# Query and key projections interleaved with windowed attention on one Trainium2 core

## The chip, the cores and the metric

The kernel runs on one core of one Trainium2 chip. Its engines are TensorE (PE in the rows: matmuls, with its weight loads as PEld), VectorE (DVE), ScalarE (ACT), GpSimd (POOL) and SyncE (SP), which here issues the DMA transfers. The metric is the device time of one execution in microseconds (us), the median of three runs.

## The reference

Two layers over 1024 latent tokens of width 1024, with 256 context tokens before them. The first layer is a gated convolution with a feed-forward part. The second is neighbourhood attention with 16 heads of width 64: the latent tokens form 16 rows of 64, and each query sees a window of 8 rows by 16 columns, with a learned bias, and all 256 context tokens.

```
qkv = hl @ w_qkv                      # 1024 latent tokens
kv_c = hc @ w_qkv[:, D:]              # 256 context tokens
...
s_win = einsum('bhqd,bhrqcd->bhqrc', q_r, k_win) * scale + bias
s_ctx = einsum('bhqd,bkhd->bhqk', q_r, k_ctx) * scale
p = softmax(concatenate([s_win, s_ctx], -1))
return einsum(p_win, v_win) + einsum(p_ctx, v_ctx)
...
yl = o @ w_o;  xl = xl + g1 * yl;  xl = xl + g2 * swiglu(...)
```

## The kernel before

Everything is float32 in and out. A projection splits weights and activations in a high and a low half and sums three products, so one output tile of 128 channels takes 8 blocks x 3 = 24 matmuls. Tokens come in tiles of 512, 512 and, for the context, 256 (`ALL`); `LAT` has the first two. The work runs in stages: modulation, convolution, feed-forward 0, then the second layer: values (`v_quarter`), queries and keys (`qk_step`), attention, output projection (`wo`), feed-forward 1.

Heads go in 8 pairs. `qk_step(i)` projects the queries (two tiles) and the keys (three tiles) of pair i, so a pair has 120 matmuls. ScalarE copies each tile out as its high half (`stage_q_hi`, `stage_k_hi`), VectorE subtracts for the low half, and SP stores both to `q_dram` and `k_dram`. All eight pairs are done before attention starts.

Attention of a pair has 8 units (four of each head; a unit is 256 queries). The keys of a unit stand in groups of 256 or less: units 0, 3, 4 and 7 have three groups, the others four, 28 in a pair, numbered here 0 to 27. Around a group TensorE does, in this order:

- in the first two groups of a unit, `scores` of the unit after the next (six matmuls),
- `turn` of the group two further on: three or four transposes of the probabilities into one of two banks; it waits for `pt_lo_done` of the group whose bank it takes,
- `values` of this group: four matmuls on `pt_hi` and `pt_lo`.

VectorE adds the bias to the scores and finds the minimum (`bias_scores`, two passes), ScalarE takes the exponentials (`probs`), VectorE inverts the sums, GpSimd multiplies (`probs` L1514), TensorE turns, ScalarE copies the high half (`pt_high`), VectorE makes the low half (`pt_low`). At the end of a unit ScalarE copies half the result (`half`), VectorE sums (`head_sum`, `sum_done`), and ScalarE and GpSimd write `o_hi` and `o_lo` (`out_high`, `out_low`) straight into the buffers that the output projection reads. The value products use banks 6 and 7 in turn, so those of a unit wait for the sum of the unit before the last.

Each engine runs its list in the written order and waits at semaphores in it. SP issues everything on one queue; `load_head(i, b)` brings the bias, queries, keys and values of one head. In its loop it waits until the scores and value products of that head of the pair before are done. The queue's order is therefore the order of the transfers.

```
def values(i, u, g):
    if g == 0:
        at_least(pe, sum_done, UNITS * i + u - 1)
```

## Time and profile before

| | |
|---|---|
| median of 3 runs | 3264.9 us (3263.08 to 3267.94) |
| the profiled execution | 3264.37 us, span 3262.6 us |
| busy: PE, PEld, DVE, ACT, POOL | 3023.7, 2499.6, 1752.1, 818.4, 741.0 us |
| instructions | 44434 |
| mean granted TensorE clock | 0.977 of full speed |
| values stage ends, q/k stage | 1758.5 us; 1759.5 to 1959.5 us |
| attention, first turn to last sum | 1985.8 to 2379.8 us |

The span is the profiled execution from its first instruction to its last. An engine is busy while an instruction of it runs; waits, branches and the issuing of DMAs don't count. In the rows, "idle before ... <-" is the time in which an engine stood still ahead of an instruction and what released it.

### The profile page before, as it was taken

The page shows a single profiled execution, that of the slowest core. Times are in us where ns is not written, and L with a number is a line of the kernel's source. Part 1 is how long each engine was busy: PE and PEld are TensorE (multiplying, and loading weights), DVE is VectorE, ACT ScalarE, POOL GpSimd, SP SyncE. Part 2 cuts the span into 40 slices and gives each one's busy share as a digit, 9 for nine tenths or more (in the row PEclk, how much of TensorE's full clock was granted, in tenths as well). Part 3 has the DMA queues.
Part 4 walks back from the last instruction along what each step waited for, and adds up shares of the span by engine and source line. Part 5 has one row for each costly group of instructions (what it writes and reads, how often), then busy time and mean ns, then how long its engine had stood idle before and what let it go on. Part 6 is the DMA issues. An engine that isn't in the chain of part 4 may idle for free. (4 is left out here: it accounts for less than half of the span.)

```text
span 3262.6 us, 44434 instructions
## 1 busy us (share of the span) xinstructions
PE 3023.7 (93%) x15712; PEld 2499.6 (77%) x15712; DVE 1752.1 (54%) x2975; ACT 818.4 (25%) x1412; POOL 741.0 (23%) x457
## 2 busy tenths in 40 slices
PE   5899999899999999999799996888898999999997
PEld 2688887578888888888499885777776888888885
DVE  1645555566677666644631115777724555555556
ACT  1311111411111111111231115777733111111112
POOL 0311211021111111111111214555531212121220
PEclk8999999999999999999999998999999999999999
DMA  9110103022221222111044327455320111111111
GB/s 350 70 52 26 51 26 87 1 73 72 77 77 54 77 72 72 63 39 39 13 101 123 139 113 159 112 118 127 81 72 13 58 39 58 39 58 39 58 39 58
DMA packets 171967, 243.97 MB, mean 75 GB/s; under 512 B 107904, under 2 KB 125312, under 8 KB 171904
## 3 DMA queue, kind: packets, MB, share of 16 engines
q1 hardware_dynamic: 171904, 243.14, 24.6%
q8 instruction: 38, 0.62, 0.1%
q14 instruction: 25, 0.20, 0.0%
HBM read 209.54 MB, written 37.49 MB: 76 GB/s over the span
## 5 line engine op out<-in xcount | busy, mean ns | idle before, releaser
L1148 DVE SCALAR_TENSOR_TENSOR residual<-psum,modulation,residual 128x512 f32<-128x512 f32 (+1 forms) x1072 | 718.1, 689 | 890.7 <-PE psum L557 889.4
L1458 POOL TENSOR_TENSOR w_lo<-raw,w_hi 128x1024 fp32r<-128x1024 f32 x196 | 491.0, 2517 | 2017.3 <-ACT w_hi L801 2017.3
L528 PE MATMUL psum<-act_hi,w_hi 128*128 128x512 f32 (+1 forms) x2528 | 676.7, 367 | 10.6 <-POOL w_lo L1458 7.6
L528 PE MATMUL psum<-act_lo,w_hi 128*128 128x512 f32 (+1 forms) x2528 | 676.7, 367 | 0.0
L528 PE MATMUL psum<-act_hi,w_lo 128*128 128x512 f32 (+1 forms) x2528 | 676.1, 367 | 0.0
L528 PEld LDWEIGHTS psum<-act_hi,w_hi 128*128 128x128 f32 x2528 | 453.5, 188 | 100.6 <-issue 7.8
L528 PEld LDWEIGHTS psum<-act_hi,w_lo 128*128 128x128 f32 x2528 | 436.4, 188 | 81.2
L528 PEld LDWEIGHTS psum<-act_lo,w_hi 128*128 128x128 f32 x2528 | 435.8, 188 | 81.5
L801 ACT ACTIVATE w_hi<-raw 128x1024 fp32r<-128x1024 f32 x196 | 203.9, 1061 | 1020.5 <-PE psum L528 964.1
L557 PE MATMUL psum<-prod_hi,w_hi 128*128 128x512 f32 (+1 forms) x1072 | 407.9, 381 | 29.7 <-DVE residual L1148 11.2
L557 PE MATMUL psum<-prod_hi,w_lo 128*128 128x512 f32 (+1 forms) x1072 | 396.4, 370 | 0.0
L557 PE MATMUL psum<-prod_lo,w_hi 128*128 128x512 f32 (+1 forms) x1072 | 395.9, 369 | 0.0
L557 PEld LDWEIGHTS psum<-prod_hi,w_hi 128*128 128x128 f32 x1072 | 202.6, 189 | 100.5 <-DVE residual L1148 35.9
L557 PEld LDWEIGHTS psum<-prod_hi,w_lo 128*128 128x128 f32 x1072 | 202.8, 189 | 36.1
L557 PEld LDWEIGHTS psum<-prod_lo,w_hi 128*128 128x128 f32 x1072 | 203.4, 190 | 21.7 <-issue 0.7
L712 PE MATMUL psum<-ident,probs 128*128 128x128 f32 x832 | 136.8, 285 | 72.9 <-DVE pt_lo L1356 42.9
L1242 DVE SCALAR_TENSOR_TENSOR mod_acc<-mod_in,silu_c,mod_acc 128x384 f32<-128x384 f32 x224 | 186.0, 876 | 0.0
L1356 DVE TENSOR_TENSOR pt_lo<-psum,pt_hi 128x512 fp32r<-128x512 f32 (+1 forms) x224 | 143.0, 649 | 56.1 <-ACT pt_hi L981 55.8
L908 ACT ACTIVATE gate<-psum 128x512 f32<-128x512 f32 (+1 forms) x110 | 54.0, 555 | 470.9 <-PE psum L528 469.8
L712 PEld LDWEIGHTS psum<-ident,probs 128*128 128x128 f32 x832 | 93.8, 143 | 98.8 <-DVE pt_lo L1356 60.8
L1167 DVE TENSOR_TENSOR prod_lo<-prod,prod_hi 128x512 fp32r<-128x512 f32 x134 | 157.8, 1224 | 9.7 <-ACT prod_hi L875 9.7
L1514 POOL TENSOR_SCALAR probs<-probs,stats 128x768 f32<-128x768 f32 (+1 forms) x128 | 119.2, 934 | 168.3 <-DVE stats L1347 166.4
(113 smaller groups left out, 3267.0 us busy)
## 6 DMA issues: line engine op xcount, KB each, us to landing
raw<-ffn_panels SPq DMA_DIRECT2D x132, 512.0 KB, 5.3
mod_raw<-mod_panels SPq DMA_DIRECT2D x48, 512.0 KB, 9.6
mod_in<-mod_rest SPq DMA_DIRECT2D x64, 384.0 KB, 3.1
raw<-conv_panels SPq DMA_DIRECT2D x32, 512.0 KB, 5.5
k_hi<-k_dram SPq DMA_DIRECT2D x32, 320.0 KB, 6.2
k_lo<-k_dram SPq DMA_DIRECT2D x32, 320.0 KB, 7.7
v_st<-v_dram SPq DMA_DIRECT2D x32, 320.0 KB, 4.1
raw<-qk_panels SPq DMA_DIRECT2D x16, 512.0 KB, 5.8
```

The lines of the kernel that those rows point to most:

```text
L528: mm = pe.matmul(psum[:, bank + b, 0:tn], w[:, s, kb, :], acts[h][:, kb, t0:t0 + tn], start=(kb == 0 and n == 0), stop=(kb == KB - 1 and n ...
L557: mm = pe.matmul(psum[:, 6 + r % 2, 0:tn], w[:, s, ob, :], h[:, t0:t0 + tn], start=(n == 0), stop=(n == 2))
L712: mm = pe.transpose(psum[:, 4 + (group0[u] + g) % 2, col:col + P], probs[:, 2 * (u % 2) + ab, start:start + P], ident[:])
L801: act.activation(panel(w_hi, s), raw[:, s], ACT.Copy).then_inc(hi_done[s], 1)
L908: act.activation(gate[:, t0:t0 + tn], psum[:, b, 0:tn], ACT.Silu).then_inc(m.a_copied, 1)
L1148: dve.scalar_tensor_tensor(out=residual[:, ob, t0:t0 + tn], in0=psum[:, 6 + r % 2, 0:tn], scalar=modulation[:, gates + ob, kind_of(t0):kin ...
L1167: dve.tensor_tensor(prod_lo[:, t0:t0 + tn], prod[:, at:at + tn], prod_hi[:, t0:t0 + tn], ALU.subtract).then_inc(m.lo, 1)
L1242: dve.scalar_tensor_tensor(out=mod_acc[:, c, :], in0=rows, scalar=by, in1=mod_acc[:, c, :], op0=ALU.mult, op1=ALU.add).then_inc(rest_acc, 1)
L1356: dve.tensor_tensor(dst, src, hi, ALU.subtract).then_inc(pt_lo_done, 1)
L1458: pool.tensor_tensor(panel(w_lo, s), raw[:, s], panel(w_hi, s), ALU.subtract).then_inc(lo_done[s], 1)
L1514: pool.tensor_scalar(probs[:, pb, 0:keys], probs[:, pb, 0:keys], stats[:, pb, 3:4], 1.0, ALU.mult, ALU.mult).then_inc(probs_done, 1)
```

## The change

The q/k stage shrinks to seven tiles: the five of pair 0 and the two query tiles of pair 1 (`FIRST_BANKS`). The other 33 tiles move into attention. `QK_CHUNKS` says which group of a pair is followed by how many of a tile's 24 matmuls: the three key tiles of the next pair behind groups 0 to 13, the two query tiles of the pair after it behind groups 15 to 25; groups 5, 10, 14, 20, 26 and 27 have none. Pair 6 has only the three key tiles, pair 7 none. `QK_DRAINED` says behind which group ScalarE and VectorE split a finished tile. All these tiles use one bank (`QK_BANK` 7), and the value products are left with one bank (`PV_BANK` 6): those of a unit now wait for the sum of the unit just before. One buffer pair of 512 columns (`stage_hi`, `stage_lo`) serves all q/k tiles, each stored on its own.

Since the activations stay in place until the last projection, `o_hi` and `o_lo` can't be written during attention. The result of a unit goes to a single staging pair (`o_st_hi`, `o_st_lo`) and is stored to `o_dram` (`store_o`), and `out_high` waits for all earlier stores to land (`o_out`). In pair 7 SP loads the results of pairs 0 to 6 back, 14 transfers of 512 KB, and after it those of pair 7. Attention's buffers are placed over the residual, which is stored before the q/k stage (8 x 512 KB) and loaded back during the output projection. The weight splits of the panels move into units 2 and 5 of a pair on ScalarE and GpSimd, and those of the first two `wo` panels into pair 6.

```diff
+        o_dram = [nc.dram_tensor(f"o_dram{n}", [PAIRS, P, TL], F32) for n in range(2)]
+        residual_dram = nc.dram_tensor("residual_dram", [KB, P, TL], F32)
...
+        QK_TILES = [(0, *tile) for tile in LAT] + [(1, *tile) for tile in ALL]
+        NQK, K_FIRST = len(QK_TILES), len(LAT)
+        QK_BANK, PV_BANK = 7, 6
+        QK_MATMULS = 3 * KB
+        FIRST_BANKS = (2, 3, 4, 5, 2, 4, 5)
...
+        QK_CHUNKS = {**chunks(1, 2, 0, (5, 5, 5, 5, 4)), **chunks(1, 3, 6, (6, 6, 6, 6)), **chunks(1, 4, 11, (8, 8, 8)),
+                     **chunks(2, 0, 15, (5, 5, 5, 5, 4)), **chunks(2, 1, 21, (5, 5, 5, 5, 4))}
+        QK_DRAINED = {6: (1, 2), 11: (1, 3), 15: (1, 4), 21: (2, 0), 27: (2, 1)}
...
+            sp.wait_ge(ffns[0].added, KB * len(ALL) * HIDDEN + 2)
+            for kb in range(KB):
+                sp.dma_start(residual_dram[kb], residual[:, kb, 0:TL]).then_inc(residual_out, 16)
...
+            def load_heads(i, b):
+                sp.wait_ge(qk_out, 32 * NQK * (i + 1))
+                at_least(sp, s_ready, 16 * i + 8 * b - 8)
...
+            def store_o(i, u):
+                h0, q0 = DH * (u // 4), 4 * (u % 4) * GRID_W
+                sp.wait_ge(o_lo_done, UNITS * i + u + 1)
+                for dram, stage in zip(o_dram, (o_st_hi, o_st_lo)):
+                    sp.dma_start(dram[i, h0:h0 + DH, q0:q0 + 2 * P], stage[h0:h0 + DH, :]).then_inc(o_out, 16)
...
+            def attention(i, panels=True, heads=True, queries=True):
+                first = isinstance(i, int) and i == 0
+                if panels:
+                    load_qk_panel(i + 2, 0)
+                    load_qk_panel(i + 2, 1)
+                elif heads:
+                    for s in range(2):
+                        load_panel("wo", s, 0, wo_panels[s])
+                load_v(i, 1)
+                if not first:
+                    store_o(i - 1, UNITS - 1)
+                if not heads:
+                    sp.wait_ge(qk_ready, NQK * PAIRS)
+                    sp.wait_ge(o_out, 32 * UNITS * (PAIRS - 1))
+                    for pair in range(PAIRS - 1):
+                        for dst, dram in zip((o_hi, o_lo), o_dram):
+                            sp.dma_start(dst[:, pair].bitcast(F32), dram[pair]).then_inc(o_most_in, 16)
+                store_o(i, 0)
+                if heads:
+                    load_bias(i + 1, 0)
+                    store_qk(i + 1, 2)
+                store_o(i, 1)
+                if heads:
+                    store_qk(i + 1, 3)
+                store_o(i, 2)
+                if heads:
+                    store_qk(i + 1, 4)
+                    load_heads(i + 1, 0)
+                    load_v(i + 1, 0)
+                store_o(i, 3)
+                if heads:
+                    load_bias(i + 1, 1)
+                store_o(i, 4)
+                if queries:
+                    store_qk(i + 2, 0)
+                if heads:
+                    load_heads(i + 1, 1)
+                store_o(i, 5)
+                if not heads:
+                    sp.wait_ge(s_ready, 2 * UNITS * PAIRS)
+                    for s in (2, 3):
+                        load_panel("wo", s, 0, wo_panels[s])
+                store_o(i, 6)
+                if queries:
+                    store_qk(i + 2, 1)
...
+            sp.wait_ge(pv_ready, UNITS * PAIRS)
+            load_residual(0)
+            load_residual(1)
+            store_o(PAIRS - 1, UNITS - 1)
+            sp.wait_ge(o_out, 32 * UNITS * PAIRS)
+            for dst, dram in zip((o_hi, o_lo), o_dram):
+                sp.dma_start(dst[:, PAIRS - 1].bitcast(F32), dram[PAIRS - 1]).then_inc(o_last_in, 16)
+            for kb in range(2, KB):
+                load_residual(kb)
...
-            def qk_step(i):
-                at_least(pe, q_lo_done, len(LAT) * i)
-                if isinstance(i, int):
-                    pe.wait_ge(v_lo_done, 4 * TOK_TILES + 4)
-                project("qk", 0, i, 0, LAT, q_ready)
-                at_least(pe, k_lo_done, len(ALL) * i)
-                project("qk", 1, i, 3, ALL, k_ready)
-            qk_step(0)
-            with pe.Fori(1, PAIRS) as i:
-                qk_step(i)
...
+            def qk_matmuls(i, tile, bank, lo, hi):
+                s, t0, tn = QK_TILES[tile]
+                if lo == 0:
+                    pe.wait_ge(lo_done[s], base["qk"][s] + i + 1)
+                for r in range(lo, hi):
+                    kb, part = divmod(r, 3)
+                    w, h = ((w_hi, act_hi), (w_hi, act_lo), (w_lo, act_hi))[part]
+                    mm = pe.matmul(psum[:, bank, 0:tn], w[:, s, kb, :], h[:, kb, t0:t0 + tn],
+                                   start=(r == 0), stop=(r == QK_MATMULS - 1))
+                if hi == QK_MATMULS:
+                    mm.then_inc(qk_ready, 1)
+            for n, bank in enumerate(FIRST_BANKS):
+                if bank in FIRST_BANKS[:n]:
+                    pe.wait_ge(qk_lo_done, n - FIRST_BANKS[:n][::-1].index(bank))
+                qk_matmuls(n // NQK, n % NQK, bank, 0, QK_MATMULS)
...
-                    at_least(pe, sum_done, UNITS * i + u - 1)
+                    at_least(pe, sum_done, UNITS * i + u)
...
-                        mm = pe.matmul(psum[:, 6 + u % 2, 0:2 * P], v_st[:, u // 4, tile, :], pt[:, slot, :],
+                        mm = pe.matmul(psum[:, PV_BANK, 0:2 * P], v_st[:, u // 4, tile, :], pt[:, slot, :],
...
+            def fill(i, group, reach):
+                ahead, tile, lo, hi = QK_CHUNKS.get(group, (reach + 1, 0, 0, 0))
+                if ahead > reach:
+                    return
+                if lo == 0:
+                    pe.wait_ge(qk_lo_done, NQK * (i + ahead) + tile)
+                qk_matmuls(i + ahead, tile, QK_BANK, lo, hi)
...
+                        fill(i, group0[u] + g, reach)
...
+            def last_pair(kb):
+                if kb == PAIRS - 2:
+                    pe.wait_ge(o_last_in, 32)
+            pe.wait_ge(o_most_in, 32 * (PAIRS - 1))
+            pe.wait_ge(sum_done, UNITS * PAIRS)
             for p in range(PAIRS):
                 at_least(pe, y_added, len(LAT) * (p - 1))
-                project("wo", p % 4, p // 4, 6 * (p % 2), LAT, y_ready, acts=(o_hi, o_lo))
+                project("wo", p % 4, p // 4, 6 * (p % 2), LAT, y_ready, last_pair, acts=(o_hi, o_lo))
...
+            def qk_high(i, n, bank=QK_BANK):
+                s, _, tn = QK_TILES[n]
+                act.wait_ge(qk_ready, NQK * i + n + 1)
+                at_least(act, qk_out, 32 * (NQK * i + n))
+                act.activation(stage_hi[:, 0:tn].bitcast(F32R), psum[:, bank, 0:tn], ACT.Copy,
+                               scale=(SCALE, 1.0)[s]).then_inc(qk_hi_done, 1)
+            for n, bank in enumerate(FIRST_BANKS):
+                qk_high(n // NQK, n % NQK, bank)
+                if n == K_FIRST - 1:
+                    split_hi("qk", 0, 1)
+                if n == NQK - 1:
+                    split_hi("qk", 1, 1)
...
+                at_least(act, o_out, 32 * (UNITS * i + u))
+                act.activation(o_st_hi[h0:h0 + DH, :].bitcast(F32R), o_sum[h0:h0 + DH, :],
+                               ACT.Copy).then_inc(o_hi_done, 1)
...
+                def drain(group):
+                    ahead, tile = QK_DRAINED.get(group, (reach + 1, 0))
+                    if ahead <= reach:
+                        qk_high(i + ahead, tile)
...
+                    if u in (2, 5) and not last:
+                        phase, n = ("qk", i + 2) if reach == 2 else ("wo", 0)
+                        split_hi(phase, (u - 2) // 3, n)
...
+            def qk_low(i, n, bank=QK_BANK):
+                s, _, tn = QK_TILES[n]
+                dve.wait_ge(qk_hi_done, NQK * i + n + 1)
+                dve.scalar_tensor_tensor(out=stage_lo[:, 0:tn].bitcast(F32R), in0=psum[:, bank, 0:tn],
+                                         scalar=(SCALE, 1.0)[s], in1=stage_hi[:, 0:tn], op0=ALU.mult,
+                                         op1=ALU.subtract).then_inc(qk_lo_done, 1)
+            dve.wait_ge(residual_out, 16 * KB)
+            for n, bank in enumerate(FIRST_BANKS):
+                qk_low(n // NQK, n % NQK, bank)
...
+                dve.wait_ge(residual_in[p], 16)
...
+                    if u in (2, 5) and not last:
+                        phase, n = ("qk", i + 2) if reach == 2 else ("wo", 0)
+                        split_lo(phase, (u - 2) // 3, n)
...
+            pool.wait_ge(o_out, 32 * UNITS * PAIRS)
+            for s in (2, 3):
```

TensorE, groups 19 and 20 of a middle pair, the end of unit 5. L712 and L826 are the turn, L729 and L843 the value products, L698 and L812 the scores, L789 the projection. Before:

```order
L712 MATMUL psum<-ident,probs 128x128 [waits probs_done,pt_lo_done]
L712 MATMUL psum<-ident,probs 128x128 x3
L729 MATMUL psum<-pt_hi,v_st 128x256 [waits pt_lo_done]
L729 MATMUL psum<-pt_lo,v_st 128x256
L729 MATMUL psum<-pt_hi,v_st 128x256
L729 MATMUL psum<-pt_lo,v_st 128x256
L34 REGISTER_ALU
L712 MATMUL psum<-ident,probs 128x128 [waits pt_lo_done]
L712 MATMUL psum<-ident,probs 128x128 x3
```

Now:

```order
L826 MATMUL psum<-ident,probs 128x128 [waits probs_done,pt_lo_done]
L826 MATMUL psum<-ident,probs 128x128 x3
L843 MATMUL psum<-pt_hi,v_st 128x256 [waits pt_lo_done]
L843 MATMUL psum<-pt_lo,v_st 128x256
L843 MATMUL psum<-pt_hi,v_st 128x256
L843 MATMUL psum<-pt_lo,v_st 128x256
L789 MATMUL psum<-act_hi,w_lo 128x512
L789 MATMUL psum<-act_hi,w_hi 128x512
L789 MATMUL psum<-act_lo,w_hi 128x512
L789 MATMUL psum<-act_hi,w_lo 128x512
L34 REGISTER_ALU
L826 MATMUL psum<-ident,probs 128x128 [waits pt_lo_done]
```

Four matmuls of the projection (the last ones of a tile) stand between the value products of a group and the next turn.

ScalarE, unit 5 of a middle pair (groups 18 to 20) and the start of unit 6. Before:

```order
L981 ACTIVATE pt_hi<-psum 128x384 [waits pt_ready]
L992 ISA [waits sum_done]
L992 ACTIVATE o_hi<-o_sum 64x256
L976 REGISTER_ALU
L981 ACTIVATE pt_hi<-psum 128x384 [waits pt_ready]
L971 REGISTER_ALU
L972 ACTIVATE probs,stats<-neg_s,stats 128x768 [waits s_done]
```

Now:

```order
L1106 ACTIVATE pt_hi<-psum 128x384 [waits pt_ready]
L34 REGISTER_ALU [waits sum_done]
L1118 ACTIVATE o_st_hi<-o_sum 64x256 [waits o_out]
L1101 REGISTER_ALU
L1106 ACTIVATE pt_hi<-psum 128x384 [waits pt_ready]
L933 ACTIVATE w_hi<-raw 128x1024 [waits raw_in1]
L1096 REGISTER_ALU
L1097 ACTIVATE probs,stats<-neg_s,stats 128x768 [waits s_done]
L1101 REGISTER_ALU
L1106 ACTIVATE pt_hi<-psum 128x512 [waits pt_ready]
L1079 ISA
L34 REGISTER_ALU [waits qk_ready]
```

The high half of the output (`out_high`) has a wait of its own, `o_out`, and a weight split and a tile's split follow close behind.

SP, the middle of a pair. Before, one head's load:

```order
L439 DMA bias_full<-bias_dram 64x896
L440 REGISTER_ALU
L440 DMA bias_full<-bias_dram 64x896
L442 ISA
L442 DMA q_st<-q_dram 64x1024 x2
L446 ISA
L446 DMA k_hi<-k_dram 64x1280 x2
L446 DMA k_lo<-k_dram 64x1280 x2
L34 ISA
L450 ISA [waits pv_ready]
L450 DMA v_st<-v_dram 128x10x64 x2
```

Now, the last key tile, the head's load and the output of unit 3 behind it:

```order
L457 DMA k_dram<-stage_hi 128x256
L457 DMA k_dram<-stage_lo 128x256
L465 REGISTER_ALU
L468 ISA [waits s_ready,qk_out]
L468 DMA q_st<-q_dram 64x1024 x2
L472 DMA k_hi<-k_dram 64x1280 x2
L472 DMA k_lo<-k_dram 64x1280 x2
L34 ISA
L478 ISA [waits pv_ready]
L478 DMA v_st<-v_dram 128x10x64 x2
L485 DMA o_dram<-o_st_hi 64x256
L485 DMA o_dram<-o_st_lo 64x256
```

The head's load waits for the store of the last key tile to land (`qk_out`), and the store of a unit's output stands behind eight loads.

## Rows read from the trace of the kernel before

**Rows 1.** Busy by stretch: PE, PEld, DVE, ACT, POOL; then PE clock, DMA share, GB/s.
```profile
1800.00:1900.00 100.00, 100.00 (x482) 83.85 (x481) 11.63 (x20) 17.35 (x28) 19.16 (x8) 1.00 0.37 137
...
2083.20:2132.00 48.80, 39.41 (x313) 36.41 (x312) 38.98 (x116) 37.20 (x77) 27.50 (x29) 1.00 0.53 120
...
2380.00:2420.00 40.00, 36.05 (x149) 29.07 (x150) 2.89 (x5) 8.45 (x11) 14.91 (x7) 0.91 0.24 79
```

**Rows 2.** Waits of PE, 2000 to 2380 us: us in total, times, longest.
```profile
PE psum L712 <- DVE pt_lo L1356: 41.8, 65, 1.4
PE psum L712 <- POOL probs L1514: 25.9, 16, 1.9
```

**Rows 3.** Timeline of SP: start, us, line; key stores, a head's load, value loads.
```profile
1936.65 0.33 SPq L420 DMA_DIRECT2D k_dram<-stage_k_hi  x1
...
1961.54 0.33 SPq L420 DMA_DIRECT2D k_dram<-stage_k_hi  x1
...
2075.28 1.12 SPq L442 DMA_DIRECT2D q_st<-q_dram  x2
...
2077.78 1.18 SPq L446 DMA_DIRECT2D k_lo<-k_dram  x2
2086.48 1.06 SPq L450 DMA_DIRECT2D v_st<-v_dram  x2
...
2185.74 1.06 SPq L450 DMA_DIRECT2D v_st<-v_dram  x2
```

**Rows 4.** Timeline of PE: 256 columns, values stage; 512 columns, q/k stage.
```profile
1757.84 0.28 PE L662 MATMUL psum<-w_lo,act_hi 128*128 128x256 f32 x1
1757.96 0.28 PE L662 MATMUL psum<-w_hi,act_hi 128*128 128x256 f32 x1
...
1762.34 0.62 PE L528 MATMUL psum<-act_hi,w_hi 128*128 128x512 f32 x2
1762.79 0.61 PE L528 MATMUL psum<-act_lo,w_hi 128*128 128x512 f32 x2
```

**Rows 5.** Timeline of PE where attention starts and where it ends.
```profile
1977.11 0.55 PE L698 MATMUL psum<-k_hi,q_st 128*128 128x256 f32 x1 [17.59 <-DMA k_lo<-k_dram]
...
1985.83 1.94 PE L712 MATMUL psum<-ident,probs 128*128 128x128 f32 x8 [3.03 <-POOL probs L1514]
...
2383.95 1.19 PE L528 MATMUL psum<-o_hi,w_hi 128*128 128x512 f32 x2 [5.03 <-POOL w_lo L1458]
```

**Rows 6.** DMA issues, 1780 to 1960 us: count, KB each, median us to landing.
```profile
k_dram<-stage_k_hi SPq DMA_DIRECT2D x7, 640.0 KB, 3.0
```

**Rows 7.** The same of 2074 to 2094 us.
```profile
k_lo<-k_dram SPq DMA_DIRECT2D x2, 320.0 KB, 7.9
v_st<-v_dram SPq DMA_DIRECT2D x2, 320.0 KB, 3.7
```

**Rows 8.** Groups by form, 2000 to 2200 us: busy us, mean ns, idle before.
```profile
L1356 DVE TENSOR_TENSOR pt_lo<-psum,pt_hi 128x512 fp32r<-128x512 f32 x82 | 56.4, 687 | 27.8 <-ACT pt_hi L981 27.8
L981 ACT ACTIVATE pt_hi<-psum 128x512 fp32r<-128x512 f32 x81 | 47.7, 588 | 9.0 <-PE psum L712 8.6
L972 ACT ACTIVATE probs<-neg_s,stats 128x768 f32<-128x768 f32 x33 | 30.9, 935 | 3.4 <-DVE stats L1341 3.3
L1365 DVE TENSOR_TENSOR o_sum<-psum,o_half 64x256 f32<-64x256 f32 x32 | 13.0, 407 | 0.5
L986 ACT ACTIVATE o_half<-psum 64x256 f32<-64x256 f32 x33 | 12.6, 382 | 1.3 <-PE psum L729 0.5
L972 ACT ACTIVATION_READ_ACCUMULATOR probs<-neg_s,stats 128x1 f32 x65 | 12.2, 187 | 0.0
```

**Rows 9.** Groups of the whole span: the weight split on ScalarE.
```profile
L801 ACT ACTIVATE w_hi<-raw 128x1024 fp32r<-128x1024 f32 x196 | 203.9, 1061 | 1020.5 <-PE psum L528 964.1
```

**Rows 10.** DMA issues, 1960 to 2000 us: count, KB each, median us to landing.
```profile
v_st<-v_dram SPq DMA_DIRECT2D x4, 320.0 KB, 10.7
```

**Rows 11.** DMA rate in 1 us slices, 2360 to 2400 us, as the output panels load.
```profile
GB/s 0 0 16 0 0 8 0 94 201 369 401 381 434 209 8 0 0 8 0 0 0 0 0 0 37 246 242 213 324 74 332 160 307 180 0 0 0 0 0 0
```

More of the change, by code:

```diff
@@ L141, in trunk @@
+        o_st_lo, nxt = place("o_st_lo", [P, 2 * P], F32, nxt)
+        o_sum, nxt = place("o_sum", [P, 2 * P], F32, nxt)
+        o_half, nxt = place("o_half", [P, 2 * P], F32, nxt)
+        assert nxt <= w_lo_end, (nxt, w_lo_end)
+        k_hi, nxt = place("k_hi", [P, 2, T], F32R, scratch_at)
+        k_lo, nxt = place("k_lo", [P, 2, T], F32R, nxt)
+        bias_inner, nxt = place("bias_inner", [P, 2, NB, GRID_W], F32, nxt)
         assert nxt <= scratch_end, (nxt, scratch_end)
-        zeros, spare = place("zeros", [P, TC], F32, spare)
@@ new lines, in _ @@
+            load_qk_panel(1, 0)
+            load_qk_panel(1, 1)
+            sp.wait_ge(bias_in, 32 * HEADS)
+            sp.wait_ge(v_ready, 4 * TOK_TILES)
+            load_bias(0, 0)
+            load_bias(0, 1)
+            for n in range(NQK):
+                store_qk(0, n)
+            for n in range(2):
+                sp.wait_ge(v_out[n], 16 * 4 * TOK_TILES)
+            sp.wait_ge(hi_done[2], base["qk"][2])
+            sp.wait_ge(hi_done[3], base["qk"][3])
+            sp.wait_ge(lo_done[2], base["qk"][2])
@@ new lines, in _, with load_residual @@
+            attention(0)
+            with sp.Fori(1, PAIRS - 2) as i:
+                attention(i)
+            attention(PAIRS - 2, panels=False, queries=False)
+            attention(PAIRS - 1, panels=False, heads=False, queries=False)
+            def load_residual(kb):
+                sp.dma_start(residual[:, kb, 0:TL], residual_dram[kb]).then_inc(residual_in[kb], 16)
+            sp.wait_ge(pv_ready, UNITS * PAIRS)
+            load_residual(0)
+            load_residual(1)
+            store_o(PAIRS - 1, UNITS - 1)
@@ L1002, in attention @@
                     pt_high(i, u, 0)
+                    drain(group0[u])
                     if more:
@@ L1016, in _ @@
             exponentials(0, 0, 1)
-            attention(0, False)
-            with act.Fori(1, PAIRS - 1) as i:
-                attention(i, False)
-            attention(PAIRS - 1, True)
+            attention(0, 2)
+            with act.Fori(1, PAIRS - 2) as i:
+                attention(i, 2)
+            attention(PAIRS - 2, 1)
+            attention(PAIRS - 1, 0)
             half(PAIRS - 1, UNITS - 1)
             out_high(PAIRS - 1, UNITS - 1)
-            for s in range(4):
+            for s in (2, 3):
                 split_hi("wo", s, 0)
@@ L1364, in head_sum, with attention, drain @@
                 at_least(dve, o_lo_done, n)
-                dve.tensor_tensor(o_sum[h0:h0 + DH, :], psum[0:DH, 6 + u % 2, 0:2 * P], o_half[0:DH, :],
+                dve.tensor_tensor(o_sum[h0:h0 + DH, :], psum[0:DH, PV_BANK, 0:2 * P], o_half[0:DH, :],
                                   ALU.add).then_inc(sum_done, 1)
-            def attention(i, last):
+            def attention(i, reach):
                 first = isinstance(i, int) and i == 0
+                last = reach == 0
+                def drain(group):
+                    ahead, tile = QK_DRAINED.get(group, (reach + 1, 0))
+                    if ahead <= reach:
+                        qk_low(i + ahead, tile)
                 for u in range(UNITS):
@@ L1493, in _ @@
                     split_lo("v", s, (quarter + 1) // 2)
-            with pool.Fori(0, PAIRS - 1) as i:
-                for s in range(2):
-                    split_lo("qk", s, i + 1)
             def tables(i, b):
```

214 lines of the change are left out of this document (92 added, 122 removed).

## The prediction

> **What bounds the kernel now.** The busy time by stretch comes first [rows 1]. In the q/k stage TensorE is busy 100.00 of 100 us, ScalarE 17.35: a projection bounds itself. In attention it is busy 39.41 of 48.8 us, VectorE 38.98, ScalarE 37.20. None is full, so a loop of waits sets the pace, and the waits of PE name it [rows 2]: 41.8 us in 65 waits for the low half of an earlier group, 25.9 us in 16 for GpSimd's probabilities, 67.7 us in 380. SP's value loads recur after 99.26 us for two pairs [rows 3], so a pair takes 49.6 us, and 67.7 x 49.6 / 380 = 8.8 us of it are idle. The ends of matmuls are modelled: a 256-column matmul is shown as 0.28 us but the next starts after 0.12 [rows 4], so each wait hides 0.16 us more, 81 / 7.66 = 10.6 waits a pair, 1.7 us. TensorE has about 10.5 us free in a pair and needs 39.1.
>
> **What can be gained at most.** The q/k stage takes 24.9 us a pair (stores of two pairs, 1936.65 and 1961.54 [rows 3]). Written singly, a 512-column matmul takes 0.45 / 2 = 0.225 us and a 256-column one 0.12 [rows 4]: 96 x 0.225 + 24 x 0.12 = 24.5 us, so the projection is no cheaper inside. One after the other a pair costs 49.6 + 24.9 = 74.5; with TensorE never waiting it costs 39.1 + 24.5 = 63.6. What matters is what lies between.
>
> **Front.** Seven tiles remain, six of 512 and one of 256 columns: 144 x 0.225 + 24 x 0.12 = 35.3 us in place of 200.0 (the stage from 1759.5 to 1959.5 in the table), -164.7. Then TensorE waited 17.59 us for the keys of head 0 [rows 5]. Now the last tile of pair 0 has the two query tiles of pair 1 behind it, 10.8 us. Its own way is longer: the single staging buffer must be free, since a store lands after 3.0 us [rows 6] and the 256-column tile is there 2.9 us after its forerunner; splits, issue and landing give 6 us to the landed store, and a head's queries and keys take 3.8 us to issue and land 7.9 us after the last issue [rows 3, 7], less 1 us since the bias is no longer ahead, about 10.8. So 6 + 10.8 - 10.8 = 6 us are left open, -11.6. A wait of 1.0 us at the stage's start goes too. Front: -177.3. The 8.7 us from the first scores to the first turn (1977.11 to 1985.83 [rows 5]) stay. The residual's store, 4 MB, lies beside the values stage: nothing.
>
> **The one value bank.** Value products of a unit now wait for: turn of its second group, high half (0.59), half (0.38) and, on VectorE, low half (0.69), a short inversion, sum (0.41) [rows 8]. Let the turn of the unit's first group start at 0. With five matmuls (1.13 us) behind both groups TensorE does turn 0.4, values 0.56, fill 1.13, turn, values, fill, scores 0.74, turn and wants the bank at 5.3. ScalarE goes exponential (0.94 + 0.19 [rows 8]), high half, exponential, high half until 3.3, half to 3.75; VectorE's sum ends at 4.7. Nothing is lost. Behind groups 5, 10, 20 and 27 a fill is missing, and other things stand in between:
> - unit 7 to 0: no fill behind 26 and 27, and a tile's split (0.59) behind 27: 2.3 us late
> - unit 1 to 2: one fill missing, a split behind 6: 1.3
> - unit 2 to 3: a fill missing, the weight split (1.06 [rows 9]) and a tile's split: 1.4
> - unit 3 to 4: ScalarE stands at the tile that ends behind 13: 0.5
>
> That is 5.5 us a pair. The least is 0: the waits of before name none of the value products for the sum [rows 2]. The most is some 12: eight boundaries at 1.5 us, the turn, high half, half and sum in a row less the scores and the turn that cover them.
>
> **The output's store behind the head's load.** Take t = 0 when VectorE has split the last key tile (behind group 15). The SP list then reads: store that tile, wait until it has landed, eight loads, store the output of unit 3. The store lands at t = 2.6; the six loads of queries and keys take 3.8 us to issue and the two of values 1.06 [rows 3], so the output's store is issued at 8.4. It lands behind what is queued: a value load lands 3.7 us after its issue alone [rows 7] and 10.7 behind others [rows 10]. The rate is an estimate: bias, queries and keys of a head, 2.29 MB, are in by 2077.78 + 0.6 + 7.9 = 2086.3 [rows 3, 7], from about 2075 on, with some 1.3 us of landing, so 230 GB/s. 2.43 MB / 230 GB/s = 10.6 us from t = 3.6 is 14.2, the output 0.5 and the landing 1.5 more: t = 16.3.
> ScalarE asks for it in unit 5 between the high halves of groups 19 and 20. TensorE starts fill 15 at t = 2.95 and would be at group 20 at 2.95 + 1.13 + 2.1 + 2.84 + 2.84 + 1.87 = 13.7 (groups 17 and 18 carry scores). ScalarE copies the output until 16.7, the high half until 17.3, VectorE the low half until 18.0: TensorE waits 4.3 us for it. Then ScalarE has weight split, exponential, high half, tile split, exponential, high half, half = 1.06 + 1.12 + 0.59 + 0.59 + 1.12 + 0.59 + 0.38 = 5.5, half ends at 22.8, the sum at 23.8 with two low operations between. TensorE wanted that bank at 15.9, so 7.9 us in all, in place of 1.4 were there no such wait (the weight split and the missing fill alone). The head's keys land at t = 13, before the scores need them at 15: no loss, by a narrow margin.
>
> By the Trainium skill ("DMA: Bandwidth & Descriptors", Queues, rings and completion order) completion isn't first in, first out per issuing engine, and a later transfer may finish its write before an earlier one. By that the output could land 2 to 3 us after its issue, at t = 11, and the region would cost 1.4 us. The rows speak against it here, with v_st at 10.7 us behind others and 3.7 alone.
>
> **Sum of a pair.** 63.6 + 5.5 + 7.9 = 77.0, and 1 us for the clock: after the 5.03 us wait at 2383.95 [rows 5] the granted clock of the next stretch is 0.91 over 40 us [rows 1], 3.6 us worth at full speed; I take 1 of 0 to 3.6. 78.0 against 49.6: +28.4, times six = +170.4.
>
> **Pair 6** has three tiles, 48 x 0.225 + 24 x 0.12 = 13.7 us, in its first half: 19.5 + 13.7 + 5 = 38.2. Its second half has no fills, so the wait for o_out finds TensorE sooner at group 20 (six groups of 1.77 = 49.6 / 28) and it ends at about 37.4: 75.6, +26.
>
> **Pair 7.** The output of its unit 0 stands behind 14 loads of 512 KB, 7.3 MB. The last stored unit of pair 6 lands at 8.5 us into the pair; at 400 GB/s [rows 11] the loads take 18.4 us, and with 3 us around them unit 0's output lands at 30. ScalarE asks for it in unit 2, eight groups of 1.77 us and a little in, at 15. The wait moves TensorE by 13 us at group 10 and 2.6 at the next sum; the other boundaries, without fills, cost some 0.4 each. +18 (0 to 20).
>
> **End.** The output projection waited 5.03 us for its weights [rows 5]. Its first panels are now split in time, it starts 4 us sooner, and waits some 2.5 us before its last channel block for pair 7's result, which goes to DRAM and back: -1.5. The residual comes back 512 KB at a time, 1.3 us each, beside 10.9 us of matmuls: nothing.
>
> Sum, against the profiled execution's 3264.4 us, which is within 0.6 of the median of the runs: 3264.4 - 177.3 + 170.4 + 26 + 18 - 1.5 = **3300 us**.
>
> **Rivals.**
> - A, faster: the output's store passes the loads, or the loads are done sooner, at both places. A pair is then 78.0 - 6.5 - 0.5 = 71.0, below 74.5: -42; pair 6 -13, pair 7 -15: 3230 us. For it: the margin is small, a landing at t = 12.5 costs nothing. Against it: the landings of [rows 7, 10]. It turns on one number, the landing. It is also where the page's rule would lead.
> - B, only pair 7's 7.3 MB make ScalarE wait: 3230 + 15 = 3245.
> - C, worse than forecast: keys land after t = 15 as well, and the clock falls after each stop: 6 x (2 + 2.6) = 28 more, 3328.
> - D, TensorE is kept full, no bank wait and no store wait: 6 x (63.6 - 49.6) + 8 - 177.3 - 1.5: 3178. ScalarE and VectorE, some 43 of 64 us each with the added splits, would allow it; the order of their lists speaks against it.
>
> **Chances.** Forecast 0.48 (its own range 3275 to 3318), A 0.18, B 0.09, C 0.17, D 0.03; 0.05 lies between B and the forecast, near no change. What a measurement can tell from none is 0.2%, 6.5 us. Faster 0.30, same 0.05, slower 0.65. The range runs from A's value to a little over C's, 3230 to 3345; it leaves out D, half of A and the end of C.
>
> **What would show it.** Right: in pairs 1 to 5 ScalarE's longest wait is at the copy to o_st_hi for o_dram, once a pair in unit 5, 5 us or more; value loads two pairs apart by some 156 us; in pair 7 a wait of over 10 us at the same line; TensorE's waits at the value products are for o_sum. Wrong: value loads 140 us apart with no DMA wait on ScalarE (A), or scores that wait for k_lo (C). The first scores should wait 6 us where they waited 17.59.

## The result and the profile after

The changed kernel takes 3277.3 us, the median of 8 runs (3271.86 to 3280.55), against 3266.0 of the kernel before: a ratio of 1.0033, 95% interval 1.0023 to 1.0044. It is slower, as forecast, by 11.3 us where 35 were forecast. The time is inside the range; the size is off by a factor of three, so the sum is what has to be looked at.

Its profiled execution has a span of 3276.2 us, 13.6 more than before. The first view is the timeline of TensorE: start, length, line, operation, and in brackets the idle time before it and what ended it. Front, a middle pair, pair 7 and the end:

```profile
1798.71 0.55 PE L812 MATMUL psum<-k_hi,q_st 128*128 128x256 f32 x1 [4.36 <-DMA k_lo<-k_dram]
1811.24 1.09 PE L826 MATMUL psum<-ident,probs 128*128 128x128 f32 x4 [2.22 <-POOL probs L1656]
...
1993.33 0.39 PE L843 MATMUL psum<-pt_hi,v_st 128*128 128x256 f32 x1 [1.16 <-DVE o_sum L1497]
2018.48 0.86 PE L826 MATMUL psum<-ident,probs 128*128 128x128 f32 x4 [4.71 <-DVE pt_lo L1488]
2023.51 0.39 PE L843 MATMUL psum<-pt_hi,v_st 128*128 128x256 f32 x1 [1.39 <-DVE o_sum L1497]
2040.71 0.35 PE L843 MATMUL psum<-pt_hi,v_st 128*128 128x256 f32 x1 [1.51 <-DVE o_sum L1497]
...
2366.34 1.12 PE L826 MATMUL psum<-ident,probs 128*128 128x128 f32 x4 [10.71 <-DVE pt_lo L1488]
...
2396.30 0.70 PE L635 MATMUL psum<-o_hi,w_hi 128*128 128x512 f32 x2 [0.97 <-issue]
2407.14 0.73 PE L635 MATMUL psum<-o_hi,w_hi 128*128 128x512 f32 x2 [1.03 <-DMA o_lo<-o_dram]
```

The first two rows answer to [rows 5]: the wait of 17.59 us for the first keys is 4.36 now, and the first turn stands at 1811.24 in place of 1985.83. In a middle pair there is one long wait, at the turn of group 22, which TensorE issues in group 20, and a wait of over half a microsecond for the sum at three of the eight units. The same waits in total, 1890 to 2268 us, five pairs (us, times, longest), against [rows 2]:

```profile
PE psum L826 <- DVE pt_lo L1488: 26.1, 9, 5.7
PE psum L843 <- DVE o_sum L1497: 23.1, 25, 1.7
```

The row names VectorE, which is only the last link. ScalarE's timeline in the same two places shows what held the high half that VectorE needs:

```profile
2016.91 0.41 ACT L1118 ACTIVATE o_st_hi<-o_sum 64x256 fp32r<-64x256 f32 x1 [8.74 <-DMA o_dram<-o_st_lo]
...
2364.91 0.42 ACT L1118 ACTIVATE o_st_hi<-o_sum 64x256 fp32r<-64x256 f32 x1 [12.35 <-DMA o_dram<-o_st_lo]
```

And SP's shows why that store is late. The last key tile's store is issued at 2000.66, eight loads follow once it has landed, then the output's store. The issue of its high half alone takes 5.30 us, so the low half, for which ScalarE waits, is issued only at 2013.94; the value loads of two pairs are 74.5 us apart where [rows 3] give 49.6 a pair:

```profile
2000.66 0.34 SPq L457 DMA_DIRECT2D k_dram<-stage_hi  x1
2003.03 1.19 SPq L468 DMA_DIRECT2D q_st<-q_dram  x2
...
2007.06 1.23 SPq L478 DMA_DIRECT2D v_st<-v_dram  x2
2008.54 5.30 SPq L485 DMA_DIRECT2D o_dram<-o_st_hi  x1
2013.94 0.54 SPq L485 DMA_DIRECT2D o_dram<-o_st_lo  x1
...
2081.58 1.29 SPq L478 DMA_DIRECT2D v_st<-v_dram  x2
```

Busy time by stretch (length, then PE, PEld, DVE, ACT, POOL, the granted clock of TensorE, DMA share, GB/s): five pairs, and 8 us around the end of the long wait in two of them, against [rows 1]:

```profile
1890.00:2268.00 378.00, 328.26 (x2160) 295.26 (x2160) 217.13 (x606) 207.61 (x416) 160.75 (x152) 0.95 0.54 138
...
2018.00:2026.00 8.00, 6.13 (x33) 5.51 (x34) 4.63 (x12) 5.50 (x11) 5.07 (x5) 0.79 0.47 128
...
2168.00:2176.00 8.00, 6.87 (x28) 5.99 (x27) 4.20 (x11) 4.67 (x11) 4.93 (x4) 0.51 0.56 159
```

After a wait of 4.7 to 5.0 us the granted clock is at its lower level, 1.2 GHz, for part of the next 8 us (0.79) or nearly all (0.51). In [rows 1] the attention of before has 1.00.

From the ends of the 64 sums (L1365 before, L1497 now) each pair's length follows, the end of its last sum less that of the pair before:

| | before | after | forecast |
|---|---|---|---|
| up to the first sum | 1996.24 | 1821.59 (-174.7) | -177.3 |
| pairs 0 to 5, mean of 1 to 5 | 49.7 | 75.5 (+154.9 in all) | 78.0 (+170.4) |
| pair 6 | 49.0 | 71.1 (+22.1) | +26 |
| pair 7 | 43.0 | 57.1 (+14.1) | +18 |
| from the last sum to the end | 882.8 | 880.0 (-2.8) | -1.5 |
| sum | | +13.6 | +35.6 |

The mean is that of pairs 1 to 5. In the total, pair 0 counts from its first sum on, units 1 to 7: 68.8 us in place of 42.8.

### The profile page after: what moved, and what is told of

It is laid out like the page before. It is cut to its first block, busy times and chain, and to the rows that moved or that the text cites. A ratio compares the mean times of both kernels' runs of the same rounds, so it can differ in the third digit from the quotient of the medians.

```text
span 3276.2 us, 44546 instructions
## 1 busy us (share of the span) xinstructions
PE 3033.8 (93%) x15712; PEld 2515.3 (77%) x15712; DVE 1761.6 (54%) x2975; ACT 817.0 (25%) x1412; POOL 737.6 (23%) x457
## 4 chain that ended last, share of the span: by engine, by line
PE 76%; DVE 6%; issue 5%; ACT 4%; SPq 4%; DMA 4%; POOL 1%; DVEq 0%; ACTq 0%; POOLq 0%
PE psum L635 42%; PE psum L664 19%; PE psum L789 4%; PE psum L769 3%; PE psum L843 2%; PE psum L610 2%; DMA o_dram<-o_st_lo 1%; PE psum L812 1%; PE psum L826 1%; DVE residual L1289 1%; SPq L485 1%; DVE prod L1269 1%; ACT probs L1097 1%; DMA mod_raw<-mod_panels 1%; ACT pt_hi L1106 1%
## 5 line engine op out<-in xcount | busy, mean ns | idle before, releaser
L635 PE MATMUL psum<-act_hi,w_hi 128*128 128x512 f32 (+1 forms) x2208 | 590.6, 367 | 9.6 <-POOL w_lo L1603 7.6
L635 PE MATMUL psum<-act_lo,w_hi 128*128 128x512 f32 (+1 forms) x2208 | 590.0, 367 | 0.0
L635 PE MATMUL psum<-act_hi,w_lo 128*128 128x512 f32 (+1 forms) x2208 | 589.5, 367 | 0.0
L635 PEld LDWEIGHTS psum<-act_hi,w_hi 128*128 128x128 f32 x2208 | 398.2, 188 | 88.7 <-issue 7.7
L635 PEld LDWEIGHTS psum<-act_lo,w_hi 128*128 128x128 f32 x2208 | 380.8, 188 | 71.0
L635 PEld LDWEIGHTS psum<-act_hi,w_lo 128*128 128x128 f32 x2208 | 380.9, 188 | 70.7
L826 PE MATMUL psum<-ident,probs 128*128 128x128 f32 x832 | 136.7, 286 | 53.1 <-DVE pt_lo L1488 50.6
L843 PE MATMUL psum<-pt_hi,v_st 128*128 128x256 f32 x448 | 141.0, 335 | 40.6 <-DVE o_sum L1497 40.4
```

What stands on the lines that cost most here:

```text
L635: mm = pe.matmul(psum[:, bank + b, 0:tn], w[:, s, kb, :], acts[h][:, kb, t0:t0 + tn], start=(kb == 0 and n == 0), stop=(kb == KB - 1 and n ...
L826: mm = pe.transpose(psum[:, 4 + (group0[u] + g) % 2, col:col + P], probs[:, 2 * (u % 2) + ab, start:start + P], ident[:])
L843: mm = pe.matmul(psum[:, PV_BANK, 0:2 * P], v_st[:, u // 4, tile, :], pt[:, slot, :], start=(g == 0 and m == 0 and part == 0), stop=(g == ...
```

## The experiments

The theory: interleaving alone gains, and the wait for the output's store, in six pairs, pair 6 and pair 7, pays it back and more. Rivals: the one value bank costs it, or TensorE's own work, or another wait stands ready behind the store's.

**One value bank alone** (before_one_bank), in the kernel before.

```diff
-                    at_least(pe, sum_done, UNITS * i + u - 1)
+                    at_least(pe, sum_done, UNITS * i + u)
...
-                        mm = pe.matmul(psum[:, 6 + u % 2, 0:2 * P], v_st[:, u // 4, tile, :], pt[:, slot, :],
+                        mm = pe.matmul(psum[:, 6, 0:2 * P], v_st[:, u // 4, tile, :], pt[:, slot, :],
```

> The kernel before with one change: the value products use bank 6 alone, so those of a unit wait for the sum of the unit just before. Theory 1 (the bank costs something at each of the 64 unit boundaries, as nothing covers the sum): in pair 7 of the changed kernel, which has no fills either, the middle units take 6.15 to 6.54 us where they took 6.0 to 6.27, so some 0.2 to 0.45 us a boundary, 13 to 29 us: 3279 to 3295 us against 3266. Rival (the loop of turn, high half and low half sets the pace and swallows it): 3266 to 3270 us.

Measured: 3273.95 us against 3267.53, ratio 1.0015 (1.0006 to 1.0024). TensorE's waits, 1830 to 2380 us:

```profile
PE psum L729 <- DVE o_sum L1365: 63.0, 60, 1.8
PE psum L712 <- DVE pt_lo L1356: 12.1, 28, 0.5
```

Both expectations missed: 6 us, between them. 63 us of new waits at the value products cost 6, since the waits at the turn for the low half fell from 41.8 [rows 2] to 12.1, and those for GpSimd's probabilities, 25.9 us in [rows 2], went with the exception of the first turn. Most of it was the same idle time, ended by another engine. A pair takes 50.2 us where it took 50.3 and 49.0 in turn, and pair 7 46.0 where it took 43.0.

**Two staging areas** (two_stagings), the single wait taken away by another buffer: the output of even units goes through partitions 0 to 63 and that of odd ones through 64 to 127.

```diff
-        o_out = sem("o_out")
+        o_out = [sem("o_out0"), sem("o_out1")]
...
-                at_least(act, o_out, 32 * (UNITS * i + u))
+                at_least(act, o_out[u % 2], 32 * (UNITS // 2 * i + u // 2))
```

> The changed kernel with two staging areas for the output in place of one (the two partition halves in turn, each with its own semaphore), so out_high waits for the stores of the unit before the last only. Theory 1 (the wait for the store behind the head's load is what the interleaving pays): the 8.5 to 10.2 us waits of ScalarE in unit 5 go, and TensorE's 4.5 to 5.7 us at the turn with them, some 5 us in each of seven pairs, and 3 in pair 7: 3277 - 38 = 3239 us, below before. Rival (another wait comes due in its place, the next head's keys or GpSimd's probabilities): no more than half of it, 3258 us or more, with a new wait of over 1 us at L812 or L826 in each pair.

Measured: 3222.81 us against 3267.53, ratio 0.9863 (0.9848 to 0.9878), 54 us below the changed kernel and 45 below before. Pairs take 68.4 us, one of them 70.0, in place of 75.5. Five pairs, 1890 to 2234 us, the waits and the stretch:

```profile
PE psum L845 <- DVE o_sum L1499: 24.9, 25, 1.6
PE psum L828 <- DVE pt_lo L1490: 1.6, 4, 0.6
```

```profile
1890.00:2234.00 344.00, 317.31 (x2164) 286.94 (x2163) 217.96 (x608) 206.84 (x416) 160.00 (x150) 1.00 0.60 151
```

The wait at the turn is gone (26.1 to 1.6), the waits for the sum stayed (23.1 to 24.9), and the clock is 1.00 where it was 0.95. In these pairs no other wait stood behind it; in pair 7 one of 5.49 us at the turn is left. A pair gains 6.8 us on the mean. 4.9 of it are the long wait. 2.2 are TensorE's busy time for the same matmuls, 65.7 us a pair at the clock of 0.95 (328.26 / 5, the first stretch in the section on the result) and 63.5 at 1.00 (317.31 / 5). The waits for the sum give 0.4 back. The expectation had only the long wait and was 16 us short, most of it in pairs 0 to 5.

**The next pair's values behind the output's store** (values_last).

```diff
                     load_heads(i + 1, 0)
-                    load_v(i + 1, 0)
                 store_o(i, 3)
                 if heads:
+                    load_v(i + 1, 0)
                     load_bias(i + 1, 1)
```

> The changed kernel with one pair of transfers moved: the next pair's values (2 x 320 KB) are issued behind the store of unit 3's output, not ahead of it. Theory 1 (the store lands behind what is queued ahead): 640 KB at 230 GB/s are 2.8 us, so ScalarE's wait falls from 9 to about 6 us and TensorE's from 5 to about 2.2, times seven: 3277 - 20 = 3257 us. Rival (a store's landing doesn't depend on what is ahead; it is the time to issue it that counts, 2 us for the two loads less): 3277 - 14 = 3263 us or less gained; with no dependence at all 3277.

Measured: 3260.03 us, ratio to before 0.9978 (0.9968 to 0.9988), 17 us below the changed kernel. Middle pairs take 71.6 to 71.9 us, 3.7 less. The two theories, 20 and 14 us, aren't far enough apart for the total to choose; the waits and the store itself do. ScalarE's wait falls from 8.9 to 6.0 us (means of pairs 1 to 5) and TensorE's at the turn from 4.9 to 2.0, so by 2.9 us each, where theory 1 had 2.8 and the rival 2; the other 0.8 us or so of the pair is busy time of TensorE at a clock of 0.98 in place of 0.95. And in this run SP isn't held at the store, which shows the landing by itself: issued behind six loads at 2001.72 us, in 0.53 us, its halves land 6.7 and 6.4 us later. The store of the next unit in the changed kernel, at 2018.30 with no load ahead, landed in 2.0:

```profile
2001.72 0.53 SPq L485 DMA_DIRECT2D o_dram<-o_st_hi  x1
```

```profile
o_dram<-o_st_hi SPq DMA_DIRECT2D x1, 64.0 KB, 6.7
o_dram<-o_st_lo SPq DMA_DIRECT2D x1, 64.0 KB, 6.4
```

So this store waited for what was queued ahead of it. Moving two transfers is enough to make the whole faster than before, by 0.2%.

**Pair 7's reloads spread** (reload_spread).

```diff
-                    for pair in range(PAIRS - 1):
+                    for pair in pairs if not heads else ():
...
                 store_o(i, 0)
+                reload(0, 1)
...
                 store_o(i, 1)
+                reload(2)
```

and so on, one pair behind each store.

> The changed kernel with pair 7's 14 reloads of 512 KB spread: four behind the store of unit 0, two behind those of units 1 to 5, in place of all ahead of unit 0's. Theory 1: ScalarE's 12.35 us wait and TensorE's 10.71 in unit 2 of pair 7 go, pair 7 falls from 57.1 to about 46: 3266 us. Rival (the reloads' traffic itself holds the pair up): pair 7 stays above 52 us, 3272 or more.

Measured: 3268.3 us, ratio 1.0006 (0.9997 to 1.0015). Pair 7 takes 46.4 us in place of 57.1. Theory 1 holds: inside pair 7 the traffic itself costs nothing that can be seen, its place ahead of one unit's stores of 2 x 64 KB cost 10.7 us. Behind it some comes back: TensorE waits 4.0 us for reloaded results in the output projection where it waited 1.0.

**Both together** (two_and_spread).

> Two staging areas and pair 7's reloads spread, both as before, together. With two staging areas alone pair 7 took 51.2 us with a 5.5 us wait of TensorE at the turn; with the spread reloads alone 46.4. Theory 1 (two separate waits, on the same store queue): pair 7 falls to 46.5 at most, 3223 - 5 = 3218 us. Rival (the reloads compete with the stores however they are placed): 3223 us.

Measured: 3222.18 us, ratio 0.987 (0.9854 to 0.9886). Pair 7 falls from 51.2 to 46.1 as theory 1 has it, 5 us, but the total shows no difference from two staging areas alone (3222.81); its runs lie between 3214.97 and 3225.84. In the profiled execution, too, the output projection waits longer for the reloaded results, 4.5 us in place of 1.4.

**A chunk behind nearly every unit's end** (covered_ends).

```diff
-        QK_CHUNKS = {**chunks(1, 2, 0, (5, 5, 5, 5, 4)), **chunks(1, 3, 6, (6, 6, 6, 6)), **chunks(1, 4, 11, (8, 8, 8)),
-                     **chunks(2, 0, 15, (5, 5, 5, 5, 4)), **chunks(2, 1, 21, (5, 5, 5, 5, 4))}
+        QK_CHUNKS = {**chunks(1, 2, 0, (5, 5, 5, 5, 4)), **chunks(1, 3, 6, (5, 5, 5, 5, 4)), **chunks(1, 4, 12, (12, 12)),
+                     **chunks(2, 0, 16, (5, 5, 5, 5, 4)), **chunks(2, 1, 22, (6, 6, 6, 6))}
```

> two_and_spread with the projection's chunks placed so that a chunk stands behind the last group of every unit but the last of a pair: groups 0 to 4, 6 to 10, 12 to 13 (12 matmuls each), 16 to 20, 22 to 25; before, nothing stood behind 10, 20 and 27. Theory 1 (one value bank costs where nothing covers the sum): the waits for the sum of 1.16 us at unit 3, 1.46 at unit 6 and 0.57 at unit 2 go, some 2.5 to 3 us a pair, 15 to 18 us: 3201 us. Rival (ScalarE's list sets these waits, through the weight splits and tile splits in units 2, 5 and 6, and a chunk only moves them): under 1 us a pair, 3213 us or more.

Measured: 3254.09 us, ratio 0.9961 (0.9948 to 0.9975), 32 us slower than with the chunks in their old places. Theory 1 falls. The rival's bound of 3213 us or more is kept, but it had no loss in it. ScalarE's timeline in group 21:

```profile
2014.09 0.58 ACT L1116 ACTIVATE pt_hi<-psum 128x512 fp32r<-128x512 f32 x1
2017.46 0.60 ACT L1091 ACTIVATE stage_hi<-psum 128x512 fp32r<-128x512 f32 x1 [2.78 <-PE psum L799]
...
2018.87 0.59 ACT L1116 ACTIVATE pt_hi<-psum 128x512 fp32r<-128x512 f32 x1
2019.48 0.38 ACT L1121 ACTIVATE o_half<-psum 64x256 f32<-64x256 f32 x1
```

The tile's split is now in the list right behind the chunk that ends the tile, and ScalarE stands 2.78 us at it with the half for the sum still ahead. TensorE's waits for the sum become 2.1 and 2.4 us at units 3 and 6, and with the first the clock drops in most pairs: unit 3 takes 9.3 us in pairs 1, 2, 4 and 5, and in pair 3, with the same wait of 2.07 us but at clock 1.00, 7.75. The two stretches, pair 2 and pair 3:

```profile
1993.00:2003.00 10.00, 9.23 (x62) 8.99 (x63) 5.90 (x19) 5.38 (x11) 6.35 (x6) 0.83 0.16 52
...
2067.00:2076.00 9.00, 7.79 (x63) 7.55 (x64) 6.43 (x19) 5.75 (x13) 6.73 (x7) 1.00 0.22 73
```

**The same with each split a group later** (late_drains).

```diff
+        QK_CHUNKS = {**chunks(1, 2, 0, (5, 5, 5, 5, 4)), **chunks(1, 3, 6, (5, 5, 5, 5, 4)), **chunks(1, 4, 13, (12, 12)),
+                     **chunks(2, 0, 17, (6, 6, 6, 6)), **chunks(2, 1, 23, (8, 8, 8))}
+        QK_DRAINED = {6: (1, 2), 12: (1, 3), 16: (1, 4), 22: (2, 0), 27: (2, 1)}
```

> covered_ends with each tile split one group later than the group that finishes it: chunks behind groups 0 to 4, 6 to 10, 13 to 14, 17 to 20, 23 to 25, splits behind 6, 12, 16, 22 and 27. In covered_ends a pair took 74.5 us where two_and_spread took 68.4; ScalarE stood 2.7 us at the tile in groups 11 and 21, and TensorE then 2.1 and 2.4 us at the sum. Theory 2 (the chunk that ends a tile must lie a group ahead of its split, since ScalarE takes the tile in its written order, ahead of the half that the sum needs): these waits fall under 0.5 us, a pair is at 67 to 69 us, the whole 3215 to 3224. Rival (it is the chunk behind groups 10 and 20 itself, or the 12 matmuls in one chunk): a pair stays above 72 us, 3240 or more.

Measured: 3229.03 us, ratio 0.9886 (0.9869 to 0.9902). 25 us of the 32 come back with the chunks behind groups 10 and 20 and the one of 12 matmuls still there, so the rival falls and the nearness of the split was the greater part of the cause. Theory 2's own numbers are missed too: the whole is above 3224, a pair takes 69.3 to 70.9 us, and the waits for the sum are not under 0.5 but 0.68 to 1.5 us at five units of a pair, 5.3 us together, no less than the five of two_and_spread (0.56, 1.16, 0.32, 1.47, 1.51; 5.0). Placing chunks moves these waits about; it has not removed them. The three pairs of 70.9 us differ from the two others in unit 0, 8.7 to 8.8 us in place of 7.25, at a granted clock of 0.81:

```profile
1951.00:1960.00 9.00, 8.49 (x44) 7.55 (x45) 5.07 (x15) 4.10 (x9) 3.39 (x5) 0.81 0.87 219
```

**The weight splits in units 1 and 4** (splits_1_4).

```diff
-                    if u in (2, 5) and not last:
+                    if u in (1, 4) and not last:
```

> two_and_spread with the weight splits of ScalarE and GpSimd at the end of units 1 and 4 in place of 2 and 5, so behind groups that have a chunk of the projection. Theory 2 (TensorE's waits for the sum of 1.16 and 1.46 us at the start of units 3 and 6 come from the 1.06 us split and the tile's split in ScalarE's list): these fall by about 1 us each, those of units 2 and 5 rise by less than 0.5: some 1.5 us a pair, 3213 us. Rival (the missing chunk alone makes them): no change, 3222 us.

Measured: 3228.95 us, ratio 0.988 (0.9863 to 0.9896). TensorE's waits in a middle pair:

```profile
1976.14 0.38 PE L853 MATMUL psum<-pt_hi,v_st 128*128 128x256 f32 x1 [1.37 <-DVE o_sum L1507]
1986.75 0.39 PE L853 MATMUL psum<-pt_hi,v_st 128*128 128x256 f32 x1 [1.16 <-DVE o_sum L1507]
2010.72 0.39 PE L853 MATMUL psum<-pt_hi,v_st 128*128 128x256 f32 x1 [1.46 <-DVE o_sum L1507]
```

1.16 and 1.46 us stay to the hundredth with the split away, so the weight split had no part in them, and theory 2 falls. The new wait at unit 2, 1.37 in place of 0.56, is what it costs at its new place; together with a unit 0 of 8.7 to 8.8 us in three pairs it makes the whole 3229 and not the rival's 3222. That the missing chunk alone makes the two waits isn't shown by this run, since the split of a projected tile stands in both places too; in late_drains, with the chunk there and the tile's split moved, they are 0.68 and 0.98, not 0.

**Nine of a tile's 24 matmuls** (fill_nine), with two staging areas (the products with a low half are left out, except the last).

```diff
+                    if bank == QK_BANK and part and r != QK_MATMULS - 1:
+                        continue
```

> two_stagings with 9 of the 24 matmuls of each tile that is projected inside attention (the high by high products and the last one; the other products are left out). Theory 1 (with the store's wait gone TensorE's own work sets a pair: 39 us of attention and 24.5 of projection, plus 4.8 of waits): a pair loses 15.3 us until the loop of before holds it, so 68.4 falls to about 54, and the whole by some 80 us, to 3143. Rival (the loop of ScalarE, VectorE and GpSimd with the added splits sets the pair already): a pair stays above 62 us, the whole above 3185.

Measured: 3159.89 us, ratio 0.9675 (0.9661 to 0.9688). Pairs take 57.6 to 60.2 us: 15.3 us of TensorE's work less gives 9.7 on the mean. Neither expectation is met. Five pairs, 1874 to 2169 us, the stretch and the waits:

```profile
1874.00:2169.00 295.00, 250.82 (x1785) 228.39 (x1785) 214.55 (x606) 204.47 (x415) 159.57 (x151) 0.97 0.70 175
```

```profile
PE psum L847 <- DVE o_sum L1501: 35.5, 34, 1.8
PE psum L816 <- DMA k_lo<-k_dram: 7.0, 5, 2.1
```

TensorE's busy time falls only by 13.3 us a pair, to 50.2 (250.82 / 5), at a clock of 0.97 in place of 1.00. Its waits for the sum are 7.1 us a pair in place of 5.0, and once a pair the scores now wait for the next head's keys, 1.4 us on the mean. So at 68.4 us TensorE's work is the larger share of the bound, not all of it.

## Why the prediction was right in sign and wrong in size

**Right.** The mechanism, its place and its moment. Take t = 0 at 2000.5, when the last key tile of that pair is split: the output's store should free ScalarE at t = 16.3, it did at 16.4; the turn should go on at 18.0, it did at 18.0; the wait should be 4.3, it was 4.71. In pair 7 the wait is there likewise, 10.7 us where 13 were forecast. Interleaving without the store's wait is worth 45 us, which only the experiment shows.

The way to t = 16.4 is the forecast one only in part, and here luck helped. The forecast had both halves of the store issued at 8.4 (its terms, 2.6 + 3.8 + 1.06, give 7.5; it was 8.0) and queued behind the loads. SP in fact stood 5.30 us at the high half, which landed 8.0 us after its start, about when the last value load did; the low half was issued at 13.4 and landed 2.9 us later. values_last, where both halves are issued at once and still land 6.4 to 6.7 us later, shows that queueing alone gives a delay of this kind.

Rival A named the rule of the Trainium skill ("DMA: Bandwidth & Descriptors", Queues, rings and completion order) that completion need not follow the order of issue. Neither here nor in values_last did the store land before the last load was about in. The same section also has a transfer's semaphore increment land only after every earlier write from that DMA engine, so a landing at t = 11 did not follow from it.

**Wrong, the sum of a pair, by 2.5 us times six: the term of the one value bank.** Means of pairs 1 to 5, term by term:

| term of a pair | forecast | measured |
|---|---|---|
| TensorE's own work (two_stagings, 317.31 / 5) | 63.6 | 63.5 |
| the one value bank, waits for the sum outside unit 5 | 5.5 | 3.3 |
| other short waits at the turn | 0 | 0.3 |
| the long wait in unit 5 | 4.3 | 4.9 |
| the wait for the sum behind it | 3.6 | 1.3 |
| the clock (65.7 less 63.5) | 1 | 2.2 |
| sum | 78.0 | 75.5 |

The step that failed is "The one value bank": 5.5 us were added up and 3.3 measured, 2.2 of the 2.5 us. All four of its lines were too large. Unit 7 to 0 waits 1.3 to 1.7 us, not 2.3; unit 1 to 2 waits 0.44, not 1.3; unit 2 to 3 1.16, not 1.4, and the weight split that it was put down to has no part in it (splits_1_4); unit 3 to 4 0.20, not 0.5.

**Wrong, the 3.6 us for the sum behind the long wait, and made good by luck.** The prediction had ScalarE's chain of 5.5 us after the stop hold TensorE again, until t = 23.8, after it had wanted the bank at 20.2. The products went on at t = 23.0 after a wait of only 1.39. TensorE reached them late by itself, at 21.6, since it ran at the lower clock after the stop: from 2018.5 to 2022.1 us the granted clock is 0.54:

```profile
2018.50:2022.10 3.60, 3.60 (x17) 3.21 (x17) 1.36 (x3) 3.60 (x8) 2.57 (x2) 0.54 0.15 36
```

So 2.3 us too much stood here, and 1.8 too little in the long wait and the clock; the region as a whole, 7.9 + 1 = 8.9 us, was measured at 8.4.

**Wrong, the first stretch and the ends.** Pair 7: ScalarE was free 25.8 us into the pair, not 30, since the first of the 14 reloads was issued 4.2 us into the pair, not 8.5; TensorE stood 10.7 us, not 13, and the 2.6 us forecast at the next sum aren't there. So 14 us and not 18. Pair 6: 71.1 us, not 75.6, and most of it is the same term as above: its first half took 34.6 us, not 38.2, with 3.0 us of waits for the sum in place of 5; its second took 36.5, not 37.4. The front gained 174.7 us, not 177.3: the wait for the keys was shorter than forecast (4.36, not 6), but a second wait of 4.28 us stands before the third set of scores, which the prediction did not have. Its chain has the same shape as that of the large one: the store of the sixth tile stands behind the first head's loads on SP, its issue takes 5.29 us, ScalarE waits 13.67 us for it to free the staging buffer, and VectorE's first bias pass is listed behind that tile's low half:

```profile
1793.41 5.29 SPq L457 DMA_DIRECT2D q_dram<-stage_hi  x1
```

```profile
1803.21 0.60 ACT L1081 ACTIVATE stage_hi<-psum 128x512 fp32r<-128x512 f32 x1 [13.67 <-DMA q_dram<-stage_lo]
```

```profile
1803.85 0.69 DVE L1437 SCALAR_TENSOR_TENSOR stage_lo<-psum,stage_hi 128x512 fp32r<-128x512 f32 x1 [13.57 <-ACT stage_hi L1081]
1804.45 0.68 DVE L1468 CUSTOM_DVE_ANT_0 neg_s<-psum,bias_full 128x512 f32<-128x512 f32 x1
```

The end: 1.03 us of wait for pair 7's result, not 2.5.

Together: -15.5 in pairs 0 to 5, -3.9 in pair 6, -3.9 in pair 7, +2.6 in front, -1.3 at the end: 22 us of the 35.6 were not there.

**The cases.** Rival A's price for a pair without the store's wait was 71.0 us, the experiment gives 68.4 (68.7 on the mean); its 3230 for the whole compares with 3222. Rival D, TensorE kept full, is nowhere seen: every interleaved version waits 4.4 us or more a pair for the sum, on the mean.

Open: no run gives the interleaved kernel a second value bank, so what its waits for the sum really cost isn't shown; in the kernel before they were mostly idle time that was there already. What makes those of units 3 and 6 is shown only so far as the weight split is ruled out. And fill_nine gains 5.6 us a pair less than it leaves out: 3.5 are new waits, and 2.0 are busy time that didn't fall, which the clock of 0.97 explains only in part.
